# Which queue issues the last tile of selected values: GpSimd's or SP's

## The reference

```
_, idx = lax.top_k(score, n_top)                       # 15 of 32 blocks of 64 past tokens, per query and group
rows = pool[phys[..., None], off, gi]                  # their keys and values, from the pages that page_table names
logits = q . rmsnorm(k) + bias;  p = masked_softmax(logits);  out = p . v
```

## Time and profile before

| | us |
|---|---|
| median of 3 runs | 1228.87 |
| the 3 runs | 1228.8, 1228.87, 1234.67 |
| the profiled execution | 1236.49 |
| its span | 1234.8 |
| TensorE busy in the span | 1178.4 (95%) |
| GpSimd busy | 221.7 (18%) |

### The profile page before, as it was taken

How to read it: one execution, slowest core, us unless ns; L and a number is a source line. 1 busy time by engine, 2 the same in 40 slices (tenths; PEclk the granted TensorE clock), 3 DMA queues, 4 the chain that set the end, 5 groups by cost and what they waited for, 6 DMA issues and landing times.

```text
span 1234.8 us, 36560 instructions
## 1 busy us (share of the span) xinstructions
PE 1178.4 (95%) x14724; PEld 976.4 (79%) x14724; DVE 477.5 (39%) x1391; ACT 278.5 (23%) x707; POOL 221.7 (18%) x376
## 2 busy tenths in 40 slices
PE   9999999999999999999788789999999999999998
PEld 7887876999999987874345457787888987978977
DVE  3111115677775333104678763441221221212214
ACT  1000003110110122325877851211011011010122
POOL 5133232011340000413355540100000000000000
PEclk9999999999999999999899989999999999999999
DMA  9999889999342464653687789599999999899821
GB/s 328 325 315 296 286 265 320 164 372 336 125 162 116 179 275 168 176 97 110 205 281 229 246 260 357 221 358 361 390 357 369 377 367 389 336 340 386 305 100 39
DMA packets 123099, 329.99 MB, mean 267 GB/s; under 512 B 17880, under 2 KB 56873, under 8 KB 121268
## 3 DMA queue, kind: packets, MB, share of 16 engines
q1 hardware_dynamic: 96772, 259.88, 57.8%
q0 software_dynamic: 16656, 59.30, 16.5%
q10 hardware_dynamic: 9504, 8.48, 2.3%
HBM read 319.16 MB, written 15.70 MB: 271 GB/s over the span
## 4 chain that ended last, share of the span: by engine, by line
PE 80%; SPq 5%; issue 5%; DMA 4%; DVE 2%; ACT 1%; POOL 1%; POOLq 1%; DVEq 0%; ACTq 0%
PE bank L2093 16%; PE bank L2792 16%; PE bank L2214 12%; PE pbank L2803 6%; PE bank L2250 6%; PE pbank L2792 3%; PE bank L2803 3%; PE bank L2151 3%; SPq L628 3%; PE bank L2339 2%; SPq L653 1%; PE bank L2744 1%; DMA gring<-in_dense_gu 1%; PE bank L2428 1%; SPq L638 1%
## 5 line engine op out<-in xcount | busy, mean ns | idle before, releaser
L2792 PE MATMUL bank<-X,gring 128*64 128x96 f32 x4608 | 196.1, 246 | 5.6 <-issue 5.6
L2792 PEld LDWEIGHTS bank<-X,gring 128*64 128x64 f32 x4608 | 192.2, 137 | 10.0 <-issue 9.9
L2093 PE MATMUL bank<-aT,gring 128*128 128x288 f32 x704 | 175.2, 407 | 1.5 <-DMA gring<-in_conv_in 1.5
L2093 PEld LDWEIGHTS bank<-aT,gring 128*128 128x128 f32 x704 | 133.0, 190 | 38.8 <-DMA gring<-in_conv_in 2.0
L2803 PE MATMUL pbank<-Q,X 128*32 128x256 f32 x1152 | 76.5, 379 | 0.0
L638 POOL DMA_DIRECT2D Q<-in_cache_cmp x96 | 52.1, 542 | 122.6 <-issue 122.6
L2214 PE MATMUL bank<-aT,gring 128*128 128x144 f32 x528 | 72.3, 286 | 1.7 <-issue 1.7
L2019 DVE TENSOR_TENSOR X<-X,bank 128x96 f32<-128x96 f32 x72 | 18.4, 256 | 134.0 <-ACT X L1341 132.2
L2214 PEld LDWEIGHTS bank<-aT,gring 128*128 128x128 f32 x528 | 67.7, 190 | 2.1 <-issue 1.8
L2012 DVE TENSOR_TENSOR hT<-hT,bank 128x288 f32<-128x288 f32 x48 | 18.9, 449 | 128.5 <-PE bank L2744 128.5
L2093 PE MATMUL bank<-Q,gring 128*128 128x288 f32 x256 | 65.0, 416 | 2.9 <-DMA gring<-in_conv_out 2.1
(11 more groups left out here) (409 smaller groups left out, 1804.2 us busy)
## 6 DMA issues: line engine op xcount, KB each, us to landing
gring<-in_moe SPq DMA_DIRECT2D x176, 512.0 KB, 5.9
Q<-in_moe SPq DMA_DIRECT2D x72, 512.0 KB, 7.1
gring<-in_dense_gu SPq DMA_DIRECT2D x44, 512.0 KB, 11.1
gring<-in_conv_in SPq DMA_DIRECT2D x24, 512.0 KB, 7.2
Q<-in_cache_cmp POOLq DMA_DIRECT2D x96, 128.0 KB, 4.3
Q<-in_cache_cmp SPq DMA_DIRECT2D x96, 128.0 KB, 4.1
gring<-in_dense_down SPq DMA_DIRECT2D x16, 704.0 KB, 5.3
Q<-in_cache_cmp ACTq DMA_DIRECT2D x64, 128.0 KB, 3.9
```

The source lines that it names most:

```text
L2093: ins = pe.matmul(bank(label, k)[:, 0:T], tile[:, 128 * i:128 * i + 128], rhs[:, i, :], start=i == 0, stop=i == C - 1)
L2792: ins = pe.matmul(m_bank(i, M_GU + f)[64 * w:64 * w + 64, CAP * u:CAP * u + CAP], gslot(("m", 0), 2 * f + u)[:, o:o + 64], ae[:, c, :], st ...
```

## The change

`by_pool` returns false for the tiles `sv` with t = 3 and b2 = 1, and the two loops that issue tiles ask `by_pool`. So for each of the 4 pairs one tile of four pages is issued by SP, with SP's semaphore.

```
         def by_pool(label):
-            return label[0] in ("sk", "sv") and label[3] == 1
+            return label[0] in ("sk", "sv") and label[3] == 1 and label[:1] + label[2:3] != ("sv", 3)
...
             for label in GN:
-                if label[0] in ("sk", "sv") and label[3] == 0:
+                if label[0] in ("sk", "sv") and not by_pool(label):
                     four_pages(sp, label, g_in)
...
             for label in GN:
-                if label[0] in ("sk", "sv") and label[3] == 1:
+                if by_pool(label):
                     if label == ("sk", 0, 3, 1):
                         masked_table(0)
```

## The result

| | before | changed |
|---|---|---|
| median | 1228.84 us (1228.16 to 1234.67, 4 runs) | 1244.53 us (1241.64 to 1252.08, 4 runs) |
| ratio of the runs | | 1.0126, 95% interval 1.0078 to 1.0174 |
| the profiled execution | 1236.49 us | 1246.56 us |
| its span | 1234.8 us | 1244.6 us |

The change is slower, as forecast: the whole interval of the ratio lies above 1, at 9.6 to 21.4 us. Forecast were 1240.6 us (+11.7 us) with a range of 1231 to 1246.4; the median came out 3.9 us above the forecast, which is less than the uncertainty of the measurement.

What follows compares the result with a forecast made beforehand. The prediction took the issuing queues of GpSimd, then SP, to bound the attention. SP's 17.5 us of added issuing, less 4.9 of waits and 0.9 of landing, gave +11.7 us: 1240.6 us, range 1231 to 1246.4.

Steps and rivals of the forecast that it cites:

- Its own sign of being wrong: At the end of the attention stage: the forecast is wrong if SP issues `pp` before 742 us; 745 to 748 expected.
- The other sign: At the end of the attention stage: the forecast is wrong if TensorE doesn't wait for `pp`; 7 to 12 us expected.
- Both queues are full at once: In the attention, 570 to 752 us: neither GpSimd's nor SP's issuing queue has room for the other's work.
- The 17.5 us of issuing, less 4.9 us of waits: On SP's queue ahead of `pp`: 16 pages at 1.09 us add 17.5 us, and waits for TensorE absorb 4.9 us.
- the slow issues: SP's issues at the 512 KB loads, 4.0 us over the plain price: bounds 0 and -4.0 us, taken as 0.
- The landing of `pp`: Transfer of `pp` at the end of the attention: 4.1 us in place of 4.96 with GpSimd done early, -0.9 us.
- The stage behind `pp` unchanged in length: Behind the landing of `pp`, TensorE's work was to keep its length, with nothing made up in the experts.
- I cost both at nothing: In the attention: TensorE's 2.86 us wait for pair 0's values and ScalarE's 3.7 us for a key tile gain nothing.
- The faster rival: In the attention: the pairs, not SP, set the end; gain 7.0 us, to 1221.9 us; chance 0.06.
- The rival of late window keys: Pair 3's softmax in the attention: late window keys move it and nothing is absorbed, 1246.4 us or above; chance 0.04.
- The rival of no difference: On SP's queue: only the load instruction costs, 0.45 us a page, giving 1229 +- 2 us; chance 0.15.

Runs made afterwards that it cites:

- the two profiles of the changed kernel: The changed kernel profiled in two separate runs against the kernel before: 1244.53 us, ratio 1.0126, and again 1243.41 us, ratio 1.0118.
- cheaper pages on both queues: Kernel before with page numbers fixed in the program for all selected tiles: 1222.03 us, ratio 0.9910; or read without bounds: 1221.89 us, ratio 0.9915.
- the kernel before with `pp` early: Kernel before with the load of `pp` issued ahead of pair 3's last tiles of values: 1231.03 us, ratio 1.0004.
- Fixed page numbers: Changed kernel with the 16 moved pages issued by page numbers fixed in the program: 1237.69 us, ratio 1.0052 to the kernel before.
- the third queue: Kernel before with the four tiles issued by ScalarE's queue: 1230.72 us, ratio 1.0001; with `pp` early too, 1231.02 us, ratio 0.9985.
- With `pp` early: Changed kernel with `pp` issued ahead of pair 3's two last tiles of values: 1234.01 us, ratio 1.0025 to the kernel before.
- filler products: Changed kernel with 20 products of constants on TensorE ahead of the twelve that need `pp`: 1243.39 us, ratio 1.0085 to the kernel before.

## Why the prediction was right, point by point

**Its own sign of being wrong came up, and misled.** It said that the forecast is wrong if `pp` is issued before 742. It was issued at 739.18 and 740.26. But that sign was in clock times of one profile, and the mark came 6.2 and 7.0 us earlier in the two profiles of the changed kernel. On the clock of the kernel before they stand at 745.4 and 747.2, within the 745 to 748 that were expected; a sign counted from the mark would have held. The other sign, no wait of TensorE for `pp`, did not come up.

**"Both queues are full at once" held.** The changed SP waits for nobody from 622 to 726 us, and cheaper pages on both queues shorten the program by 0.9%.

**The 17.5 us of issuing, less 4.9 us of waits, held**: +12.6 expected, +10.6 and +12.4 measured in the two profiles. Of the slow issues, for which I bounded a gain of 4.0 us and took 0, some went in the first profile: the window loads at 629.74 took 0.91 us where the earlier trace rows have 1.90. Both differences are to one profile of the kernel before. In the kernel before with `pp` early, the issue at 110.2 us and the four pages that moved behind it, 4.4 us, give 114.6 in place of 117.2 (an estimate), so the delay is known only to 2 or 3 us. Fixed page numbers show that it is issuing, not bytes.

**The landing of `pp` held**: 4.1 expected, and 743.19 - 739.18 = 4.0 and 744.54 - 740.26 = 4.3 us measured.

**"The stage behind `pp` unchanged in length" failed.** The sum had a term too few: the twelve products behind the wait ran at the 1.2 GHz level and took 2.2 and 2.9 us more. With it both sums close. In the first profile it is 10.6 - 1.0 + 2.2 = 11.8 us, as measured; that this is almost the forecast's 11.7 is luck, since the missing term made up for 2.0 us less of delay. In the second it is 12.4 - 0.7 + 2.9 = 14.6, and its stage is 149.5 - 134.7 = 14.8 us longer. The term has the size and the sign of what the medians lie above the forecast, but the runs are too uncertain to show that it is this.

**"I cost both at nothing" held for the time.** TensorE's 2.86 us wait for pair 0's last values went, while it waited 1.62 and 2.67 us for values of later pairs; nothing of this reached the end. The other wait, ScalarE's for selected keys, didn't end with GpSimd's relief: it grew from 4.9 to 12.6 us, because SP's tiles were late. The faster rival failed on SP's lack of room, as was said. What GpSimd's relief would be worth where SP isn't burdened stays open, since on the third queue ScalarE's own delay of 4.8 us stands against it.

**The rival of late window keys was given 0.04 and was half right.** Window keys did come late (5.6 us of ScalarE's waits), and so did selected keys, which I hadn't named. The pairs' chain grew by 2.8 us in the profile. It didn't decide, because TensorE waited longer for `pp`. With `pp` early some of it should remain, but the 2.6 us by which the two ratios differ there are within their uncertainty.

**The rival of no difference fell** with every run of the changed kernel. By the rule of the Trainium skill, "DMA: Bandwidth & Descriptors", "Issuing engines are not separate DMA queues", issuing time is usually small beside the DMA. Here 1.09 us beside a landing time of 3.0 us was enough to bound a stage, as 128 pages stand on each queue, and a smaller price per page shortened it; the measurement decides.

## What to carry to other kernels

Before work is moved from one issuing queue to another, count the time between the starts of its issues, the reads and checks of registers included, and look for what the receiving queue issues last ahead of a consumer that is already waiting: that one load bears the whole sum. If both queues are full, making an issue cheaper brings what moving it can't; here two checking instructions per page were worth 0.9%. A third queue isn't free either: ask what its engine has to compute behind the issues. And a new wait of TensorE has a second price behind it, in the products that run at the lower clock.

## What the runs showed of the hardware that I had not expected

- An idle TensorE costs again after it wakes. Behind waits of 7.2 and 9.3 us twelve products took 5.4 and 6.1 us in place of 3.2, at a granted clock of 0.56 and 0.50. Behind waits of 2.4, 3.7 and 7.4 us they took 4.9 us, at 0.63 to 0.65, so the price doesn't follow the length of the wait alone. Behind a wait of 0.4 us, or behind filler products, they took 3.1 to 3.2 us.
- The two instructions that check a page number (0.15 and 0.02 us in the trace) cost 0.29 us per page between starts on SP and 0.24 us on GpSimd, more than their own durations: 1.09 to 0.80 and 1.14 to 0.90.
